# Low parts of gather rows by a product with minus identity, and later shared and gate products, in a two-layer MoE decoder kernel

## The reference

```
scores = sigmoid(h @ w_router)                    # 256 tokens x 64 experts
chosen = top 6 experts of the 4 best groups of 8, by scores + bias
w      = scores of the chosen, normalised, x 2.5
routed = sum over the chosen of  w * (silu(h @ Wg[e]) * (h @ Wu[e])) @ Wd[e]
shared = (silu(h @ Sg) * (h @ Su)) @ Sd
x      = x + g2 * (routed + shared)               # g2: a gate row from the adaLN projection
```

## Time and profile before

| what | value |
|---|---|
| three timed runs | 1295.25, 1295.28, 1299.4 us; median 1295.28 |
| the profiled execution's own time | 1298.68 us |
| its span, first to last instruction | 1296.9 us |
| mean granted TensorE clock | 0.941 |
| TensorE (PE) busy | 1098.4 us, 85% of the span |
| VectorE (DVE) busy | 495.6 us, 38% |
| ScalarE (ACT) busy | 249.6 us, 19% |
| moved by DMA | 502.25 MB, mean 387 GB/s |

### The profile page before, as it was taken

One profiled execution on the slowest core, in us unless ns is written; L12 is line 12 of the kernel. 1 busy time (PEld: TensorE's weight loads), 2 busy tenths in 40 slices (PEclk: granted clock), 3 DMA queues, 4 the chain that ended last, 5 costly groups with the idle time before them and its releaser, 6 DMA issues.

```text
span 1296.9 us, 17378 instructions
## 1 busy us (share of the span) xinstructions
PE 1098.4 (85%) x6680; PEld 610.0 (47%) x6680; DVE 495.6 (38%) x1108; ACT 249.6 (19%) x574; POOL 0.4 (0%) x5
## 2 busy tenths in 40 slices
PE   5999899998788798787859999999878878878785
PEld 4887477454234234243327577745423433423332
DVE  1297774432313132212227877543231313221231
ACT  2021623111101011111112482311110101111110
POOL 0000000000000000000000000000000000000000
PEclk9999899999799889899989999999988999889998
DMA  9999987999999999999989757799999999999996
GB/s 348 378 402 409 361 321 309 381 423 421 425 424 423 423 423 424 423 423 424 423 314 391 312 196 264 286 379 424 422 424 423 423 423 424 423 423 423 425 423 278
DMA packets 101337, 502.25 MB, mean 387 GB/s; under 512 B 12009, under 2 KB 37510, under 8 KB 46982
## 3 DMA queue, kind: packets, MB, share of 16 engines
q1 hardware_dynamic: 100790, 500.92, 95.1%
q10 hardware_dynamic: 464, 0.20, 0.1%
HBM read 500.04 MB, written 1.05 MB: 386 GB/s over the span
## 4 chain that ended last, share of the span: by engine, by line
SPq 52%; PE 31%; DMA 7%; DVE 5%; issue 4%; ACT 1%; DVEq 0%; ACTq 0%
SPq L585 45%; PE bank L739 23%; SPq L684 3%; DMA ring<-in_moe_w_down 3%; SPq L592 3%; PE bank L1177 2%; PE bank L742 2%; DMA ring<-in_moe_w_gate_up 2%; PE bank L841 1%; PE bank L983 1%; DMA w_gu<-in_ada_w 1%; DMA ring<-in_ada_w 1%; DVE w_dn L1627 1%; PE bank L1158 1%; PE bank L906 1%
## 5 line engine op out<-in xcount | busy, mean ns | idle before, releaser
L739 PE MATMUL bank<-w_gu,ring 128*32 128x512 f32 (+1 forms) x1120 | 296.1, 700 | 109.8 <-DMA w_gu<-in_moe_w_gate_up 35.7
L739 PEld LDWEIGHTS bank<-w_gu,ring 128*32 128x32 f32 (+1 forms) x1120 | 78.7, 132 | 277.9 <-issue 277.6
L1844 DVE TENSOR_TENSOR hh<-sg,bank 128x256 f32<-128x256 f32 x44 | 27.4, 623 | 414.4 <-ACT sg L1445 414.4
L739 PE MATMUL bank<-w_gu_x,ring 128*32 128x512 f32 (+1 forms) x352 | 160.1, 666 | 8.4 <-DMA ring<-in_moe_w_gate_up 5.8
L739 PE MATMUL bank<-ring 128*32 128x512 f32 (+1 forms) x272 | 142.9, 675 | 9.9 <-DMA gate<-in_moe_w_gate_up 5.3
L739 PE MATMUL bank<-w_gu,hhT 128*32 128x512 f32 (+1 forms) x416 | 138.3, 596 | 9.4 <-DMA ring<-in_moe_w_down 7.6
L739 PE MATMUL bank<-w_dn,ring 128*32 128x512 f32 x240 | 118.3, 795 | 8.0 <-DMA w_gu_x<-in_moe_w_gate_up 8.0
L1445 ACT ACTIVATE sg<-bank 128x256 f32<-128x256 f32 x44 | 16.9, 384 | 497.9 <-PE bank L739 497.9
L1861 DVE SCALAR_TENSOR_TENSOR bank<-bank,w_slot,gate 128x512 f32<-128x512 f32 x88 | 66.8, 759 | 103.7 <-PE bank L739 103.7
L739 PE MATMUL bank<-ring,hhT 128*32 128x512 f32 (+1 forms) x208 | 87.4, 596 | 1.2 <-DVE hhT L1851 0.6
L739 PE MATMUL bank<-sel,h_hi 128*128 128x256 f32 x352 | 87.8, 290 | 0.0
(11 more groups left out here) (299 smaller groups left out, 1687.6 us busy)
## 6 DMA issues: line engine op xcount, KB each, us to landing
w_gu<-in_moe_w_gate_up SPq DMA_DIRECT2D x130, 1024.0 KB, 25.6
w_gu<-in_moe_w_down SPq DMA_DIRECT2D x46, 1024.0 KB, 26.4
w_gu_x<-in_moe_w_gate_up SPq DMA_DIRECT2D x40, 1024.0 KB, 26.0
ring<-in_ada_w SPq DMA_DIRECT2D x36, 1024.0 KB, 10.1
ring<-in_moe_w_gate_up SPq DMA_DIRECT2D x34, 1024.0 KB, 26.3
w_dn<-in_moe_w_gate_up SPq DMA_DIRECT2D x28, 1024.0 KB, 26.2
ring<-in_moe_w_down SPq DMA_DIRECT2D x22, 1024.0 KB, 26.3
w_dn<-in_moe_w_down SPq DMA_DIRECT2D x14, 1024.0 KB, 26.0
```

Source lines behind the costliest of these rows:

```text
L739: return nc.tensor.matmul(o, a, b, start=first, stop=last)
L1844: v.tensor_tensor(hh[:, :].rearrange("s (f p) -> s p f", f=FE // P), sg[:, :].rearrange("s (p f) -> s p f", f=FE // P), bank[b][:, FE:2 * ...
```

## The change

The banks are filled by TensorE in the turned order already (`turned_rows`), so that ScalarE's copies to `h_hi` read and write runs of 64. The low parts are no longer VectorE's: TensorE adds minus `h_hi` onto each bank, by one product with a negated identity (`low_part`), and four more ScalarE copies make `h_lo`. The two gate products of layer 1 and most of the shared gate product, two of its first eight products and all of the second eight, come behind `gate_up(0)`; ScalarE's Silu of it comes behind its `silu(0)`. The product for the order waits for `routing` (raised right after `hot`) and no longer for the flags. VectorE makes `neg_ident` at the start of `experts` and does the two gate additions just before the passes' loop. SP's program is not touched.

```diff
         def interleaved(h, j):
-            return h[:, j // 2, :, :].rearrange("t k (c q) -> t c q k", c=KT)[:, 4 * (j % 2):4 * (j % 2) + 4, :, :]
+            return h[:, j // 2, :, 64 * (j % 2):64 * (j % 2) + 64]
         def in_order(ps):
-            return ps[:, :].rearrange("t (c q k) -> t c q k", c=4, k=KT)
+            return ps[:, :].rearrange("t (k x) -> t k x", k=KT)
+        def turned_rows(j, c):
+            return bank[j][:, :].rearrange("t (k c q) -> t c q k", k=KT, c=4)[:, c, :, :]
...
-                if n == 3:
-                    gate_half(3, 0)
-                    gate_half(3, 1, 6)
...
-                        last = tr(bank[j][:, k * P:(k + 1) * P], hT[:, 4 * half + k, ti * P:(ti + 1) * P])
+                        last = nc.tensor.matmul(turned_rows(j, k), hT[:, 4 * half + k, ti * P:(ti + 1) * P], const("ident"),
+                                                start=k == 0, stop=True, is_transpose=True, skip_group_check=True)
...
-                pe.wait_ge(sem("gate_sb"), 6 * l + 2)
-                shared_gate_up(0, 0, 6)
+                def low_part(j):
+                    pe.wait_ge(sem("h_act"), 8 * l + j + 1)
+                    nc.tensor.matmul(bank[j][:, :], neg_ident[:, :], interleaved(h_hi, j), start=False,
+                                     stop=True, skip_group_check=True).then_inc(sem("h_ps"), 1)
+
+                pe.wait_ge(sem("gate_sb"), 4 * l + 2)
+                shared_gate_up(0, 0, 6, 0, 2)
+                pe.wait_ge(sem("routing"), 2 * l + 1)
+                for j in range(4):
+                    low_part(j)
+                    shared_gate_up(0, 0, 6, j + 2, j + 3)
                 pe.wait_ge(sem("chosen"), l + 1)
...
-                shared_gate_up(0, 1, 6)
...
-                pe.wait_ge(sem("h_act"), 4 * l + 4)
-                pe.wait_ge(sem("h_dve"), 4 * l + 4)
+                pe.wait_ge(sem("h_act"), 8 * l + 8)
                 gather_half(0, 0)
                 gather_half(0, 1, (2, 3))
-                pe.wait_ge(sem("tables_sb"), 3 * l + FLAGS_SB)
+                pe.wait_ge(sem("routing"), 2 * l + 2)
                 mm(bank[1][0:1, 0:E], const("row")[0:E, :], hot[:, :], True, True).then_inc(sem("tables_ps"), 1)
                 gate_up(0)
+                if l == 1:
+                    gate_half(3, 0)
+                    gate_half(3, 1, 4)
+                shared_gate_up(0, 0, 6, 6, KT)
+                shared_gate_up(0, 1, 6)
+                pe.wait_ge(sem("tables_sb"), 3 * l + FLAGS_SB)
 
                 pe.wait_ge(sem("w_of"), l + 1)
                 pe.wait_ge(sem("sh_g"), l + 1)
```

On ScalarE and VectorE:

```diff
                 for j in range(4):
-                    act.wait_ge(sem("h_ps"), 4 * l + j + 1)
+                    act.wait_ge(sem("h_ps"), 8 * l + j + 1)
                     copy(interleaved(h_hi, j), in_order(bank[j])).then_inc(sem("h_act"), 1)
+                for j in range(4):
+                    act.wait_ge(sem("h_ps"), 8 * l + 4 + j + 1)
+                    copy(interleaved(h_lo, j), in_order(bank[j])).then_inc(sem("h_act"), 1)
...
+                gathered(0, 0)
+                gathered(0, 1, (2, 3))
+                silu(0, GU_BANK[0])
                 after(("sgu", l, 0))
                 nc.scalar.activation(sh_g[:, :, :].rearrange("p f n -> p (f n)"), bank[6][:, :], ACT.Silu)\
                     .then_inc(sem("sh_g"), 1)
...
+                v.tensor_scalar(neg_ident[:, :], const("ident"), -1.0, None, ALU.mult).then_inc(sem("routing"), 1)
...
-                for j in range(4):
-                    dve.wait_ge(sem("h_act"), 4 * l + j + 1)
-                    v.tensor_tensor(interleaved(h_lo, j), in_order(bank[j]), interleaved(h_hi, j).bitcast(F32), ALU.subtract)\
-                        .then_inc(sem("h_dve"), 1)
-
...
-                v.tensor_scalar(hot[:, :], const("rank_of", E), rank[:, 0:1], None, ALU.is_equal)
+                v.tensor_scalar(hot[:, :], const("rank_of", E), rank[:, 0:1], None, ALU.is_equal).then_inc(sem("routing"), 1)
...
+                if l == 1:
+                    gate_half(3, 0)
+                    gate_half(3, 1, 4)
                 dve.wait_ge(sem("gate_sb"), 4 * l + 4)
...
             norm(3, ((3, 72, hT),))
-            gate_half(3, 0)
-            gate_half(3, 1, 6)
             experts(1)
```

More of the change, by code:

```diff
@@ L328, in build @@
             sg = sb("sg", [P, FE], scope=moe)
+            neg_ident = sb("neg_ident", [P, P], F32R, scope=moe)
             with ExitStack() as picks:
@@ L913, in experts, with shared_gate_up @@
                     for k in range(4):
-                        last = tr(bank[j][:, k * P:(k + 1) * P], hT[:, 4 * half + k, ti * P:(ti + 1) * P])
+                        last = nc.tensor.matmul(turned_rows(j, k), hT[:, 4 * half + k, ti * P:(ti + 1) * P], const("ident"),
+                                                start=k == 0, stop=True, is_transpose=True, skip_group_check=True)
                     last.then_inc(sem("h_ps"), 1)
-                def shared_gate_up(j, f, b):
+                def shared_gate_up(j, f, b, k0=0, k1=KT):
                     w = use(("sgu", l, j))
-                    for k in range(KT):
+                    for k in range(k0, k1):
                         last = mm(bank[b][:, f * N:(f + 1) * N], w[:, k, f * P:(f + 1) * P], hT[:, k, :], k == 0, k == KT - 1)
@@ L1455, in experts @@
                     .then_inc(sem("sh_g"), 1)
-                gathered(0, 0)
-                gathered(0, 1, (2, 3))
-                silu(0, GU_BANK[0])
                 act.wait_ge(sem(f"hh_ready{l}"), 1)
```

## The result

The changed kernel took 1309.51 us (median of 6 runs, 1306.21 to 1314.52) against 1295.87 us of the kernel before on the same chip (6 runs, 1294.66 to 1299.4): ratio 1.0092, 95% interval 1.0068 to 1.0116. It is slower by 0.9%, 3.7 us above the forecast median of 1305.8 and 0.5 us inside the upper end of the forecast range, 1299.5 to 1310.0. The profiled execution took 1308.59 us with a span of 1306.7; the prediction's sum for it was 1309.2. Of the twelve executions of the kernel with the low parts alone (e10), one took 1402.98 us at a mean granted clock of 0.746 and is left out of that kernel's ratio.

What follows compares the result with a forecast made beforehand. The prediction took SP's expert weight loads, and holes in front of their full stream, as the bound. Layer losses of 5.0 and 5.5 us added to 1295.28 gave 1305.8 us, range 1299.5 to 1310.

Steps and rivals of the forecast that it cites:

- main case: Late release of unit 14's slot delays the load stream in both layers: 1305.8 us, own range 1303.5 to 1308.5, chance 0.77.
- slow transposes: Rival: stepped bank writes double the transposes' 1.92 us, adding 1.9 ahead of each release; 1309.6 us, chance 0.07.
- Low parts: Between `chosen` and `slot_of`: VectorE's subtractions leave, gather starts 2.7 us earlier; four added TensorE products cost 0.1 on the path.
- ScalarE: Four more copies, each taken at 0.60 us rather than 0.93; last low copy near 210.2; stepped bank writes taken at 0.
- the low parts don't come off the path: Rival with copies at 0.93 us: gather leads by only 2.3, 1306.6 us; inside the main case, no separate chance.
- Gate-up: Layer 0: starts 4.13 us after the gather's first product, lasts 7.02, now from 216.1 to 223.1.
- Shared product: Ten products, 4.36 us, behind gate-up: unit 14's slot freed 12.8 us late, at 227.75, with fourteen loads queued behind.
- What the late start costs: Release to fifteenth landing: 39.4 to 41.3 us, middle 40.4; layer 0 loses 5.0 us (4.0 to 5.9).
- TensorE behind it: Tables' transposes wait for ScalarE's Silu, start about 228.45; TensorE 2.6 us late through `down(1)`, hidden by the loads.
- Only TensorE's delay counts: Rival: loads catch up and `down(1)` binds again; 2.6 plus 2.6 to 4.0, sum 5.9, 1301.2 us, chance 0.11.
- Gate products of layer 1: 1.7 us leave the front but return ahead of the release, again 12.8 late; layer 1 loses 5.5 us (4.5 to 6.4).
- The gather's lead carries through: Faster rival between gather and `down(1)`: earlier gate-up halves free units sooner, gain 7.1 us, 1288.2 us, chance 0.05.

Runs made afterwards that it cites:

- e10: Changed kernel with shared products, their Silu and gate halves put back, leaving only low parts by TensorE and ScalarE's copies; 1299.46 us, ratio 1.0008 to the kernel before.
- e5: Changed kernel with all shared gate products moved to pass 4 and unit 14 loaded behind the order; 1301.96 us, ratio 1.0025 to the kernel before.
- e8: e5 with six unread products added in TensorE's idle time ahead of the gather; 1298.03 us, ratio 1.0004 to the kernel before.
- e6: Kernel before, its low parts still VectorE's, with all shared gate products moved to pass 4; 1309.74 us, ratio 1.0077.
- e7: Changed kernel with only the second eight shared gate products moved to pass 4; 1301.76 us, ratio 1.0027 to the kernel before.
- e9: e7 with the gate halves of layer 1 back in front of the logit products; 1302.01 us, ratio 1.0034 to the kernel before.
- e11: e8 with the gate halves of layer 1 in front of the logit products; 1298.44 us, ratio 1.0002 to the kernel before.

## Why the prediction was right, by its steps

The mechanism was right: the slot released 12.8 us late, the fourteen loads behind it, the lateness of TensorE hidden. The nearness of the numbers is in part luck. The median of 1309.51 lies above the main case's own range of 1303.5 to 1308.5, and by its number alone it would speak for the slow transposes (1309.6), which the trace rules out; without the room kept for that rival the range would have been missed by 1.0 us. The 1309.2 for the profiled execution was met to 0.6 us because a front that came out 4.4 us shorter without an edit hid stages 1.4 us longer than forecast and 2.3 us more between them.

*Low parts.* Right: the gather leads by 2.71 us (forecast 2.7). The low products stand 0.66 apart with one eighth, two passes of 0.22, between them; so about 0.22 each is left for them by this sum, near the scatter's 0.24 in the earlier trace rows.

*ScalarE.* Right. One copy to `h_hi` took 0.60 us (mean 603 ns), as taken. The prediction set this length of one beside 3.73 / 4 = 0.93, a share of four copies that overlap. Like by like, one copy took 1.09 us before, and by the same division it is now 2.06 / 4 = 0.52:

```profile
L1335 ACT ACTIVATE h_hi<-bank 128x512 fp32r<-128x512 f32 x4 | 3.7, 1092 | 0.2 <-PE bank L742 0.2
L1350 ACT ACTIVATE h_hi<-bank 128x512 fp32r<-128x512 f32 x4 | 2.1, 603 | 0.2 <-PE bank L915 0.2
```

The last low copy ended at 205.43, 2.1 us ahead of the gather, so the rival in which the low parts don't come off the path falls. So does that of the slow transposes: with their stepped writes the sixteen took 1.92 us, as in the earlier trace rows.

*Gate-up.* Right: from the gather 4.10 (4.13), gate-up 7.02.

*Shared product.* Right, and the step that decides: release and issue came 27.02 us from the logits, forecast 27.04; in layer 1 it was 28.74. The late load alone, on the kernel before, gave 1.0091.

*What the late start costs.* Here is the size that was off. From the first issue to the fifteenth landing it was 41.0 and 41.2 us, not the middle of 40.4 but near the high end of 41.3 (in the repeat of the changed kernel 40.8 and 42.0). The first load was not slow: it landed 4.80 after its issue in both layers. But one landing of each row came late against the 2.46 of the earlier trace rows: in layer 0 the one at 242.02, 3.85 us behind the one before, and in layer 1 the second, 4.0 behind the first. A break of that kind is in the trace of before too (246.40, 3.93 behind). It is no hole in the stream, for the DMA engines are full through that of layer 0:

```profile
240.00:241.00 1.00, 1.00 (x11) 0.90 (x10) 0.93 (x3) 0.60 (x1) 0.00 (x0) 1.00 0.99 418
241.00:242.00 1.00, 1.00 (x10) 1.00 (x9) 0.94 (x4) 0.00 (x0) 0.00 (x0) 1.00 1.01 426
```

What makes it stays open. So the loss is +5.55 and +6.3 in place of 5.0 and 5.5.

*TensorE behind it.* Right as to its size (2.60 late at `down(1)` in layer 0, forecast 2.6) and right that the loads hid it: unit 14 moved back in the list leaves about this rest, 0.29% (5.1 us in the two stages, where TensorE is 5.8 us late). *Only TensorE's delay counts*, the rival with 5.9 us and 1301.2, is thus near what remains when the late load is taken away.

*Gate products of layer 1.* As forecast, they shift from one side of the release to the other; with them in front the time is the same. Of the 1.4 us that VectorE's late additions might cost TensorE, its trace has one wait of 0.5.

*The gather's lead carries through.* It did not, and could not with SP held: the halves of gate-up 0 ended 2.7 us early and SP stood at the semaphore for 26.5 us in layer 0.

*Sum.* 10.5 us forecast, 11.9 found in the two stages. In the timed runs the ratio of 1.0092 makes 11.9 us of 1295.87 too, while the two medians stand 13.6 apart; the rest is inside the ratio's interval (8.8 to 15.0 us).

*The rules weighed.* The first load took 4.80 us in both layers. That is between the 5.0 of the earlier trace rows and the 4.4 estimated from the page "DMA: Bandwidth & Descriptors" of the Trainium skill (section "Anatomy of one DMA"), whose fit is for transfers issued by GpSimd, while these are SP's. The 358 GB/s of its section "Specifications", there half of what a memory stack gives to two cores, was again passed by one core alone, with 423.

## What to carry to other kernels

Before a product is moved, look up which semaphore its last instruction raises and where the waiting transfer stands in the list of the queue that issues it: here ten products of 4.36 us, no work saved on TensorE either way, held up fourteen loads in each layer and cost 11.9 us. In a kernel whose end is set by its loads, a gain on another engine has to reach the transfer queue to count. And before an idle time is emptied further, look at the granted clock of what follows: here it fell, and products without a use in that time kept it up at no cost that the trace shows.

## What was not expected of the hardware

TensorE's granted clock fell after a stretch that was short. Behind the 2.36 us of waiting ahead of the ranking products in e5, the next four microseconds ran at 0.50 of full clock and the four behind them at 0.64; gate-up(0) came 2.5 us (layer 0) and 1.6 us (layer 1) later than with six unread products there (e8, busy for 4.86 of 5 us, clock 1.00), in otherwise the same program. Both layers of e5 and e6 show such a fall there, and none of those with products in that time (e7, e8, e9, e11).

ScalarE's copy of a bank of 128 x 512 to float32r took 1.09 us (four in 3.73) where it wrote element by element in the turned order, and 0.60 us (four in 2.06) where it wrote runs of 64; the bank was read in its own order both times. TensorE paid nothing for making the turned order in its transposes: 1.92 us for sixteen, before and after.
